# Weight sums of a fast matrix product: two DMA transfers and VectorE in place of GpSimd

## The reference, cut to what matters

```
x = x + 0.5 * _swiglu(_rms_norm(x, norm_ffn[l]), w_gate[l], w_up[l], w_down[l])
def _swiglu(x, w_gate, w_up, w_down):              # w_gate, w_up: 1024 x 2816, w_down: 2816 x 1024
    return (jax.nn.silu(x @ w_gate) * (x @ w_up)) @ w_down
```

## Time and profile before

| | |
|---|---|
| median of the runs | 1645.57 us |
| the profiled execution | 1640.43 us, of it the span 1638.5 us |
| granted TensorE clock, mean | 0.938 |
| TensorE busy | 1391.6 us (85%) |
| VectorE busy | 1295.6 us (79%) |
| ScalarE busy | 861.1 us (53%) |
| GpSimd busy | 511.4 us (31%) |
| moved by DMA | 230.79 MB, mean 141 GB/s |

### The profile page before, as it was taken

How to read it: one execution, slowest core, us unless ns; L and a number is a source line. 1 busy time by engine, 2 the same in 40 slices (tenths; PEclk the granted TensorE clock), 3 DMA queues, 4 the chain that set the end, 5 groups by cost and what they waited for, 6 DMA issues and landing times.

```text
span 1638.5 us, 22438 instructions
## 1 busy us (share of the span) xinstructions
PE 1391.6 (85%) x8981; PEld 1152.4 (70%) x8981; DVE 1295.6 (79%) x1228; ACT 861.1 (53%) x1066; POOL 511.4 (31%) x250
## 2 busy tenths in 40 slices
PE   6788889999758888767888999994788799999997
PEld 5566668987546666645666898783566689878886
DVE  5988876667788888688878776679888867599877
ACT  5455556565544555544555665553455545466554
POOL 8333310086353332253332004907333303300000
PEclk8899999999879999978999999996998999999999
DMA  7444436121444443434442722122444377346541
GB/s 277 154 154 154 154 108 200 46 80 53 154 139 147 154 156 118 154 109 168 154 153 83 225 96 79 41 73 106 172 153 153 131 228 236 104 159 209 197 137 68
DMA packets 129539, 230.79 MB, mean 141 GB/s; under 512 B 4687, under 2 KB 69895, under 8 KB 129189
## 3 DMA queue, kind: packets, MB, share of 16 engines
q1 hardware_dynamic: 126960, 223.75, 40.3%
q10 hardware_dynamic: 1877, 5.59, 0.9%
q0 software_dynamic: 608, 0.12, 0.0%
HBM read 228.39 MB, written 2.63 MB: 141 GB/s over the span
## 4 chain that ended last, share of the span: by engine, by line
PE 49%; DVE 28%; ACT 7%; issue 7%; DMA 5%; POOL 4%; ACTq 0%; POOLq 0%; SPq 0%; DVEq 0%
PE bank L524 33%; DVE w_gate L1152 6%; PE bank L911 4%; DVE down_lo L1119 4%; DVE up_lo L509 3%; DMA w_up<-in_ffn_w_gate_dram 3%; DVE gate_lo L1119 3%; DVE extra_lo L1119 3%; PE bank L915 2%; PE bank L1957 2%; DVE work L1161 2%; DMA w_gate<-in_ffn_w_up_dram 1%; POOL xg L1270 1%; POOL xg L1276 1%; ACT extra_hi L1011 1%
## 5 line engine op out<-in xcount | busy, mean ns | idle before, releaser
L1254 POOL TENSOR_TENSOR mix<-w_gate 128x2048 f32<-128x2048 f32 x20 | 100.9, 5043 | 403.6 <-DMA w_gate<-in_ffn_w_up_dram 403.6
L524 PE MATMUL bank<-down_hi,hT 128*128 128x512 f32 (+1 forms) x352 | 137.9, 453 | 66.4 <-DVE down_lo L1119 36.7
L524 PEld LDWEIGHTS bank<-down_hi,hT 128*128 128x128 f32 x352 | 77.5, 221 | 90.7 <-issue 42.9
L524 PE MATMUL bank<-extra_hi,hT 128*128 128x512 f32 x256 | 96.4, 440 | 41.1 <-DVE work L1136 24.3
L524 PE MATMUL bank<-up_hi,ff_hi 128*128 128x512 f32 x288 | 118.9, 413 | 13.0 <-DVE up_lo L509 13.0
L1260 POOL TENSOR_TENSOR w_gate<-mix,w_up 128x2048 f32<-128x2048 f32 x20 | 93.3, 4663 | 99.4 <-DVE down_lo L1119 44.8
L1152 DVE TENSOR_TENSOR w_gate<-w_gate,w_up 128x2048 f32<-128x2048 f32 x20 | 122.8, 6138 | 0.0
L524 PE MATMUL bank<-up_lo,ff_hi 128*128 128x512 f32 x288 | 115.5, 401 | 0.0
L524 PE MATMUL bank<-up_hi,ff_lo 128*128 128x512 f32 x288 | 115.2, 400 | 0.0
L509 DVE TENSOR_TENSOR up_lo<-w_down,up_hi 128x2048 fp32r<-128x2048 f32 x36 | 100.4, 2789 | 11.6 <-ACT up_hi L504 11.6
L1263 POOL TENSOR_TENSOR w_up<-w_gate,w_up 128x2048 f32<-128x2048 f32 x20 | 93.4, 4670 | 48.6 <-DVE gate_lo L1119 22.6
(11 more groups left out here) (460 smaller groups left out, 4316.4 us busy)
## 6 DMA issues: line engine op xcount, KB each, us to landing
w_down<-in_ffn_w_down_dram SPq DMA_DIRECT2D x44, 1024.0 KB, 5.4
w_up<-in_ffn_w_up_dram SPq DMA_DIRECT2D x24, 1024.0 KB, 5.3
w_gate<-in_ffn_w_gate_dram SPq DMA_DIRECT2D x23, 1024.0 KB, 5.1
w_gate<-in_ffn_w_up_dram SPq DMA_DIRECT2D x20, 1024.0 KB, 5.8
w_up<-in_ffn_w_gate_dram SPq DMA_DIRECT2D x20, 1024.0 KB, 5.2
w_up<-in_w_in_dram SPq DMA_DIRECT2D x12, 1024.0 KB, 9.1
w_gate<-in_w_up_dram SPq DMA_DIRECT2D x11, 1024.0 KB, 5.0
w_up<-in_w_up_dram SPq DMA_DIRECT2D x11, 1024.0 KB, 5.1
```

The source lines that it names most:

```text
L524: mm = pe.matmul(out_, lhs(l_), rhs(r_), start=first and i == 0, stop=last and i == 2, **kw)
L1254: inc(pool.tensor_tensor(T_FROM["mix"], slot["gate0"][:, :], slot["gate1"][:, :], add))
```

## The change

GpSimd makes no sums in the feed-forwards. T1 is now put into `mix` by two transfers of 1 MB from GpSimd's queue: the first copies the quarter of `w_gate` from DRAM, the second, issued when the first has landed, adds the quarter of `w_up` onto it (`accum_op=ALU.add`). Both start as soon as the low part of P5 of the step before has been taken. The slots are filled as before, so these 2 MB of a step are read from DRAM twice.

VectorE makes the other sums: `sum_2` (where `sum_3` was), and `sum_3` and `sum_4` behind the low parts of P6 and P5, the down tile and `gate_0`, ahead of the low part of P7. It makes the eight activation sums too (`x_whole`, `x_sums`). The low part of P2 of the first step is taken ahead of the halves of the first group. ScalarE's high part of P7 waits for `sum_3` as before. `gn_rows` is merged into `head_inv`, which makes room for the semaphore `t1_in`; counts follow.

```
-SUMS = {P5: 1, P6: 2, P4: 3}
+SUMS = {P6: 1, P7: 2, P4: 3}
...
             def p2(s):
                 if s > 1:
-                    added(4 * s - 6)
+                    added(3 * s - 5)
                 else:
                     pe.wait_ge(S["summed"], 4 * f + 3 + past["summed"])
                 quarter_product(s, P2, 2, own_half(0, 1), True)
...
                 sl = T_SLOTS[i]
-                if i in SUMS:
+                if i == P5:
+                    act.wait_ge(S["t1_in"], 32 * s + 160 * f + past["t1_in"])
+                elif i in SUMS:
                     act.wait_ge(S["t_sum"], 3 * (s - 1) + SUMS[i] + 15 * f + past["t_sum"])
-                elif i == P7:
-                    act.wait_ge(S["c_added"], 4 * s - 3 + 20 * f + past["c_added"])
                 else:
...
+            def sums(n):
+                dve.wait_ge(S["t_sum"], n + 15 * f + past["t_sum"])
+
+            def sum_2(s):
+                dve.wait_ge(S["t1_in"], 32 * s + 160 * f + past["t1_in"])
+                dve.wait_ge(loaded["up1"], uses.now("up1", s - 1) * 16)
+                dve.wait_ge(S["t_split"], 3 * s - 2 + 15 * f + past["t_split"])
+                dve.tensor_tensor(slot["gate0"][:, :], T_FROM["mix"], slot["up1"][:, :], ALU.add).then_inc(S["t_sum"], 1)
+
             def sum_3(s):
-                dve.wait_ge(S["t_sum"], 3 * s - 2 + 15 * f + past["t_sum"])
-                dve.wait_ge(loaded["up1"], uses.now("up1", s - 1) * 16)
+                dve.wait_ge(loaded["gate1"], uses.now("gate1", s - 1) * 16)
                 dve.tensor_tensor(slot["gate1"][:, :], slot["gate1"][:, :], slot["up1"][:, :], ALU.add)\
-                   .then_inc(S["c_added"], 1)
+                   .then_inc(S["t_sum"], 1)
+
+            def sum_4(s):
+                sums(3 * s - 2)
+                dve.wait_ge(S["t_split"], 3 * s - 1 + 15 * f + past["t_split"])
+                dve.tensor_tensor(slot["up0"][:, :], slot["gate0"][:, :], slot["up0"][:, :], ALU.add).then_inc(S["t_sum"], 1)
+
+            def x_whole(k):
+
+                for t in range(NT):
+                    h_ready(dve, n_norm, 4 * k + 3)
+                    quarter_ = [hT[p_][:, 4 * k:4 * k + 4, t * P:(t + 1) * P].bitcast(F32) for p_ in range(2)]
+                    dve.tensor_tensor(xg[t, k], *quarter_, ALU.add).then_inc(S["x_sums"], 1)
+
+            def x_sums():
+
+                for n, (to, one, two, op) in enumerate((((1, 1), (1, 1), (1, 0), ALU.subtract), ((1, 0), (0, 0), (1, 0), ALU.subtract),
+                                                        ((0, 0), (1, 1), (0, 0), ALU.add), ((0, 1), (0, 0), (0, 1), ALU.subtract))):
+                    dve.wait_ge(S["x_sums"], 4 + n + 8 * f + past["x_sums"])
+                    dve.tensor_tensor(xg[to], xg[one], xg[two], op).then_inc(S["x_sums"], 1)
...
             low_of(1, P1)
+            low_of(1, P2)
             sum_half(1, 0)
             sum_half(1, 1)
             dve.wait_ge(S["row_mm"], f + 1 + past["row_mm"])
@@ -1187,8 +1215,10 @@
             gate_ = whole[:, 0, :].rearrange("p (j n) -> p j n", j=2)
             dve.tensor_tensor(gate_, gate_, rms_row.unsqueeze(1).broadcast_to([P, 2, SEQ]), ALU.mult)\
                .then_inc(S["gate_scaled"], 1)
-            low_of(1, P2)
+            x_whole(0)
             first_hidden()
+            x_whole(1)
+            x_sums()
             low_tile(0)
...
-                sum_3(s)
+                sum_2(s)
                 low_of(s, P6)
                 if s == 1:
                     gate_0(s)
@@ -1209,6 +1239,8 @@
                 if s > 1:
                     low_tile(2 * s - 2)
                     gate_0(s)
+                sum_3(s)
+                sum_4(s)
                 low_of(s, P7)
...
-        def pool_layer_ffn(pool, uses, f, n_norm, front=False):
-            add, sub = ALU.add, ALU.subtract
-
-            def inc(ins):
-                ins.then_inc(S["t_sum"], 1)
-
-            def sums(n):
-                pool.wait_ge(S["t_sum"], n + 15 * f + past["t_sum"])
-
-            def staged_(n):
-                if n + 15 * f + past["t_split"]:
-                    pool.wait_ge(S["t_split"], n + 15 * f + past["t_split"])
-
-            def landed(sl, more):
-                pool.wait_ge(loaded[sl], uses.now(sl, more) * 16)
-
-            def t1(s):
-                staged_(3 * s - 3)
+        def pool_layer_ffn(pool, uses, f, l, wg, wu):
+            for s in range(1, SUPER + 1):
+                if 3 * (s - 1) + 15 * f + past["t_split"]:
+                    pool.wait_ge(S["t_split"], 3 * (s - 1) + 15 * f + past["t_split"])
                 if f and s == 1:
                     pool.wait_ge(S["mix_low"], 5 + past["mix_low"])
-                landed("gate0", s)
-                landed("gate1", s - 1)
-                inc(pool.tensor_tensor(T_FROM["mix"], slot["gate0"][:, :], slot["gate1"][:, :], add))
-
-            def others(s):
-                landed("up1", s - 1)
-                staged_(3 * s - 2)
-                sums(3 * s - 2)
-                inc(pool.tensor_tensor(slot["gate0"][:, :], T_FROM["mix"], slot["up1"][:, :], add))
-                staged_(3 * s - 1)
-                sums(3 * s - 1)
-                inc(pool.tensor_tensor(slot["up0"][:, :], slot["gate0"][:, :], slot["up0"][:, :], add))
-
-            def x_sums():
-
-                for n, (t, k) in enumerate(((0, 0), (1, 0), (0, 1), (1, 1))):
-                    h_ready(pool, n_norm, 4 * k + 3)
-                    quarter_ = [hT[p_][:, 4 * k:4 * k + 4, t * P:(t + 1) * P].bitcast(F32) for p_ in range(2)]
-                    pool.tensor_tensor(xg[t, k], *quarter_, add).then_inc(S["x_sums"], 1)
-                pool.wait_ge(S["x_sums"], 4 + 8 * f + past["x_sums"])
-                for n, (to, one, two, op) in enumerate((((1, 1), (1, 1), (1, 0), sub), ((1, 0), (0, 0), (1, 0), sub),
-                                                        ((0, 0), (1, 1), (0, 0), add), ((0, 1), (0, 0), (0, 1), sub))):
-                    if n:
-                        pool.wait_ge(S["x_sums"], 4 + n + 8 * f + past["x_sums"])
-                    pool.tensor_tensor(xg[to], xg[one], xg[two], op).then_inc(S["x_sums"], 1)
-
-            if front:
-                x_sums()
-            t1(1)
-            if not front:
-                x_sums()
-            others(1)
-            for s in range(2, SUPER + 1):
-                t1(s)
-                others(s)
-            uses.layer_ffn()
+                to = T_FROM["mix"].rearrange("p (c n) -> p c n", n=512)
+                pool.dma_start(to, quarter(wg, l, 0, s)).then_inc(S["t1_in"], 16)
+                pool.wait_ge(S["t1_in"], 32 * s - 16 + 160 * f + past["t1_in"])
+                pool.dma_start(to, quarter(wu, l, 0, s), accum_op=ALU.add).then_inc(S["t1_in"], 16)
+                pool.wait_ge(S["t1_in"], 32 * s + 160 * f + past["t1_in"])
...
-                pool_layer_ffn(pool, uses, 0, 0, front=l == 0)
+                pool_layer_ffn(pool, uses, 0, l, a["ffn1_w_gate"], a["ffn1_w_up"])
                 pool.wait_ge(S["params_ready"], 1 + past["params_ready"])
                 pool_mixer(pool, link)
-                uses.tiles()
-                uses.out()
-                pool_layer_ffn(pool, uses, 1, 2)
+                pool_layer_ffn(pool, uses, 1, l, a["ffn2_w_gate"], a["ffn2_w_up"])
```

More of the change, by code:

```diff
@@ L172 @@
 SIGNALS = {
-    "head_sum": 4, "head_root": 4, "head_inv": 2, "head_rows": 2, "head_spread": 4, "keys_ready": 2, "cl_stat": 2,
+    "head_sum": 4, "head_root": 4, "head_inv": 4, "head_rows": 2, "head_spread": 4, "keys_ready": 2, "cl_stat": 2,
     "gain_ready": 1, "rows_picked": 2, "params_psum": 2, "params_ready": 1,
@@ L176 @@
     "diag_ready": 2, "row_mm": 2, "gate_scaled": 2,
-    "x_sums": 16, "a_high": 8, "a_low": 8, "t_sum": 30, "t_high": 30, "t_split": 30, "p_copied": 30,
-    "c_added": 40, "ff_turned": 20,
+    "x_sums": 16, "t1_in": 10 * 32, "a_high": 8, "a_low": 8, "t_sum": 30, "t_high": 30, "t_split": 30, "p_copied": 30,
+    "c_added": 30, "ff_turned": 20,
     "h_high": 24, "h_low": 24, "prod_done": 22, "ff_high": 22, "mix_high": 5, "mix_low": 5, "gu_mm": 4,
@@ L187 @@
     "pav_mm": 2, "pav_done": 2, "mat_mm": 2, "mat_done": 2, "sa_mm": 4, "sa_done": 4, "st_mm": 3, "st_done": 3,
-    "cend_ready": 1, "y_mm": 2, "y_sq": 2, "y_gated": 2, "gn_rows": 2,
+    "cend_ready": 1, "y_mm": 2, "y_sq": 2, "y_gated": 2,
     "mixr_ready": 2, "score_mm": 6, "biased": 6, "maxed": 6, "exp_done": 12, "p_ready": 6, "pt_mm": 6, "pt_done": 6,
@@ L230, in build @@
         names = """head_sum head_root head_inv head_rows head_spread keys_ready cl_stat gain_ready rows_picked params_psum params_ready mu_ready half_done squares_done
-            half_mean rms_root normed diag_ready row_mm gate_scaled x_sums a_high a_low t_sum t_high t_split
+            half_mean rms_root normed diag_ready row_mm gate_scaled x_sums t1_in a_high a_low t_sum t_high t_split
```

(22 more changed lines are left out.)

## The result

The kernel after takes 1679.58 us (two runs, 1679.12 and 1680.04), against 1645.57 before: 1.021 of it, interval 1.018 to 1.024. Predicted were 1655.6 (1604 to 1712): the direction and the range held, the loss is 34 us and not 10. The profiled execution has a span of 1678.2 us.

The account below looks back on a forecast made before the run. Bound: the order of work on VectorE and ScalarE and `up0`'s landing. Three later feed-forwards gain 3.4 us each, the front loses 20.4: +10 on 1645.6 gives 1655.6 us, range 1604 to 1712.

Parts of the forecast that it names:

- The blocking by GpSimd: VectorE's `sum_3` and low part of P4 wait out GpSimd's sums; removing this frees 8.0 us per period.
- The new place of the weight sums: `sum_4` comes later on VectorE, so five fills burst behind it; ScalarE waits 4 us or more before P2's high part.
- X: Time the adding transfer occupies the DMA engines: 5.4 us, twice a plain 1 MB transfer; ends 2.7 and 8.1.
- The constant of the first loop: Loop from `sum_4` through five fills and `up0`'s landing to the next `sum_4`: 37.1 us, plus the adding transfer's time.
- The head start of 1.4 us: Between P5's low part and the fills: the addition moves 7.0 us after that part, 1.4 before the first fill.
- The second loop: Loop without transfers, from `sum_3` through P7's high part, TensorE's P5 to transposes, and back to `sum_3`: 38.6 us.
- the rival without sharing: GpSimd's transfers don't slow SyncE's fills at all; the loop without transfers governs, 38.6 to 39: about 1590, chance 0.06.
- The front: First feed-forward: the adding transfer delays P2's weights beyond 32.0; first feed-forward loses 20.4 us (6.9 to 33.9).
- The later starts: Three later feed-forwards: P2's weights landing to first `sum_4` takes 31.9 us; each feed-forward gains 3.4.
- Adding at the price of a copy: Rival: the addition costs the DMA engines no more than copying, 2.7 to 4 us; 1610 to near 1620, chance 0.22.
- The slow addition: Rival: the addition holds the engines during the five-fill burst, delaying P2's high part; 1701 at 8.1 us, chance 0.30.

Follow-up runs that it names:

- 1: The kernel after, with T1's second transfer a plain copy instead of an addition: 1629.5 us, 0.992 of before.
- 4: The kernel after with no transfers for T1; VectorE makes T1 too, directly ahead of `sum_2`: 1659.9 us, 1.010 of before.
- 7: The kernel after, with `sum_3` moved ahead of the low part of P5 on VectorE: 1678.7 us, 1.022 of before.
- 3: The kernel after, with GpSimd holding the adding transfer back until `up0` has landed: 1646.2 us, 1.001 of before.
- 6: The kernel after with the down tile's fill ahead of SyncE's wait for `t_sum` and the addition held until `up0` landed: 1645.6 us, 1.001 of before.
- 8: The kernel after with tile fill first, addition held until `up0` landed, and `sum_3` ahead of P5's low part: 1615.2 us, 0.983 of before.
- 2: The kernel after, with SyncE issuing the step's down tile ahead of its wait for `t_sum`: 1642.6 us, 0.999 of before.
- 12: The kernel after with tile fill first, `sum_3` and `gate_0` early, addition not held: 1694.5 us, 1.031 of before.
- 10: The kernel after with tile fill first, addition held, `sum_3` early and `gate_0` directly behind P6's low part: 1620.4 us, 0.986 of before.

## Why the prediction was right in direction and too small

- **The blocking by GpSimd.** Right: 6.2 to 6.35 us became 2.28 to 2.29 throughout.
- **The new place of the weight sums.** Right: the fills come in a burst behind `sum_4`, ScalarE waits 4.7 us ahead of P2's high part (forecast 4 or more), TensorE 5.2 to 7.1 us before P5 (about 6).
- **X.** Right by itself, 5.3 us alone for the forecast 5.4; beside fills 5.7 (periods of 1) to 6.1 (one step of it), so 0.3 to 0.7 more.
- **The constant of the first loop: the step that failed.** I had `up0` landing 14.5 + X = 19.9 after `sum_4`; it was 21.6. The head start of 1.4 us is what was wrong. Its estimate had the addition moving 7.0 us after P5's low part. That low part ended at 573.26 and the addition was issued at 579.72, 6.5 later, but until 583.0 the queues show packets of fills alone: it begins to move 10 us after the low part. The fills move from about 581.6, 1.1 us after `sum_4` (forecast 1.2). So the addition had no lead over the fills; it starts more than a microsecond behind them, and all of it falls between `sum_4` and `up0`. With head start 0 the sum is 15.9 + 5.4 = 21.3, and with X at 5.7 it is 21.6. Why an issued addition takes over 3 us to begin, where the copy took 1.5, no run shows; its issue takes 1.28 us on GpSimd for the copy's 0.77. The way from there to the next `sum_4` was 22.4 for 22.6.
- **What is left of the period.** 21.6 + 22.4 = 44.0 is the second feed-forward. The first and third are 0.7 us longer, at the same issues and rates: `up0` lands 11.5 us after its issue at 848.05, against 10.4 here. Up to that landing 0.4 MB more of fills were moved than here (5.9 MB for 5.5), which is 1 us at 400 GB/s; why they came in between was not found.
- **The second loop.** Wrongly sized: 38.6 forecast, some 41 by 4 (43 less its extra sum). In after it cost nothing (7). By it the rival without sharing, 1590, could not have come either: it needed 39, and 2 us in sixteen periods are 32.
- **A wait left out.** My first loop let the fifth fill follow the fourth. In the traces `up0` is not issued until the low part of P4 is done, 11.2 us after `sum_4` in after. This cost nothing only because the engines were full until then; that the sum comes out without it is luck. In 3, 6 and 8 it is part of the chain.
- **The front.** Landing at 36.7 for 32.0 + 5.4 = 37.4, the first `sum_4` done at 68.0 for 69.3. Right; the loss of 28.6 for 20.4 comes from the four loops behind it, 2.4 us longer each.
- **The later starts.** From P2's landing to the first `sum_4` 31.4 us for 31.9 (second feed-forward). Right; gains of 3.4 became losses of 1.6, 3.6 and 6.2, which is 5.0, 7.0 and 9.6 for four loops. The longer loops give 6.4, 9.2 and 6.8; the differences, up to 2.8 us either way, I did not trace.
- **The rivals.** Adding at the price of a copy is excluded by 1; it would have given what 1 gives, 1629. The slow addition was the right mechanism at the right place (2, 3), at X below 6.8; a constant 1.7 too small did what a larger X would have done. That the engines would not be shared is excluded by the two queues' packets in the same stretch and by `up0`'s 10.4 us.
- **The Trainium skill** (Collectives: The Full Stack, bandwidth ceiling: the adding step of a collective reads two sources and runs at about half the rate of the copying one, 1.93). The runs agree for this transfer too: 399 GB/s for fills, 187 to 207 for the addition alone. The Trainium skill, DMA: Bandwidth & Descriptors, "Issuing engines are not separate DMA queues" (transfers of all queues share the 16 engines): the trace agrees, 260 to 274 GB/s at a share of 1.09 with both queues at work, about what equal bytes at 399 and 197 make (264).

## What to carry to other kernels

An addition in a DMA wasn't free here: it filled the engines for as long as two copies, and what it cost depended on who waited for a transfer in that stretch. Ask when its bytes begin to move, not when its condition is met; here 1.4 us of assumed lead, 16 times, was most of the error (22 of 32 us in the periods). Before crediting an engine with being freed, take apart what rides along: the activation sums alone gained 18 us, and the weight sums were best on VectorE with `sum_3`, `gate_0` and a fill put in better places. Whether GpSimd's own sums would gain as much from these places was not run. When a loop is shortened, know the next one to within a microsecond, and count the half clock that TensorE had here behind waits of 3 to 7 us.

## What I had not expected

- An issue on GpSimd takes 0.77 us for the 1 MB copy and 1.28 us for the addition (SyncE: 0.37), and in the step looked at its bytes begin to move more than 3 us after that issue's start; from issue to landing it takes 9.75 us even when held back from the burst, where a fill takes 5.5.
- Products behind 6 to 7 us of idle TensorE run at a granted clock of 0.50: 12 matmuls in 5.5 us instead of 2.7. After P5's start at 581.36 the clock is 1.00 again from 588. In the kernel before, P5 started at 557.54 behind 3.2 us of idle, and the clock was 0.50 from 558 to 560.
- The same kernel with one wait more is 74 us faster (12 to 10), the largest difference of the study: beside four other fills and the addition one fill took 15.2 us.
